# Reordering loads, state updates and the last copies in the SSD layer of a two-layer decoder step

## The reference

```python
def ssd_mixer(h, conv_state, ssm_state, ...):
    proj = h @ w_in                       # z (2048), xbc (3072), dt (32)
    conv = silu(conv_b + sum_k xpad[:, k:k + t] * conv_w[k])
    dt = softplus(dt_raw + dt_bias)
    # per chunk and head: decay from cumsum(dt * a), y = (C B^T * decay) @ (x dt) + C state
    new_state = state * exp(cum[:, -1]) + einsum('bsgrp,bsgn->bgrpn', xdt * to_end, bm)
    y = (y + d_skip * xs) * silu(z)
    y = y * rsqrt(mean(y * y, -1) + 1e-5) * norm_g      # mean over each of 4 groups of 512
    return y @ w_out, new_conv_state, new_state
```

## Time and profile before

| what | value |
|---|---|
| median of 3 runs | 1172.66 us |
| runs | 1162.14 to 1172.76 us |
| the profiled execution | 1171.1 us, span 1169.3 us |
| PE busy | 1051.3 us (90%) |
| DVE / ACT / POOL busy | 469.3 / 297.0 / 133.3 us |
| mean granted TensorE clock | 0.945 |
| SSD stage | 0 to 300 us |
| tail 0, from norm to gated embedding | 300 to about 617 us |

### The profile page before, as it was taken

How to read it: one execution, slowest core, us unless ns; L and a number is a source line. 1 busy time by engine, 2 the same in 40 slices (tenths; PEclk the granted TensorE clock), 3 DMA queues, 4 the chain that set the end, 5 groups by cost and what they waited for, 6 DMA issues and landing times. The chain is left out here.

```text
span 1169.3 us, 14744 instructions
## 1 busy us (share of the span) xinstructions
PE 1051.3 (90%) x5243; PEld 658.4 (56%) x5243; DVE 469.3 (40%) x1383; ACT 297.0 (25%) x765; POOL 133.3 (11%) x121
## 2 busy tenths in 40 slices
PE   7899998698799999899799989779989999989868
PEld 5688775587554444344477875345755344444347
DVE  2769898932331112011355977472161111111132
ACT  2211798700321111111220015362051011101031
POOL 0000013300001000000004724452000000000000
PEclk9899998799988999999999998889988999999989
DMA  8744696675959999999556975949368899999901
GB/s 287 248 163 149 220 278 215 198 281 198 399 225 408 427 429 428 425 427 428 213 216 235 339 262 178 370 136 382 128 265 370 363 427 426 428 428 426 417 4 38
DMA packets 88943, 347.36 MB, mean 297 GB/s; under 512 B 14690, under 2 KB 52578, under 8 KB 72322
## 3 DMA queue, kind: packets, MB, share of 16 engines
q1 hardware_dynamic: 81186, 313.57, 69.3%
q10 hardware_dynamic: 5376, 24.40, 5.3%
q0 software_dynamic: 2304, 8.39, 1.8%
HBM read 331.66 MB, written 23.04 MB: 303 GB/s over the span
## 5 line engine op out<-in xcount | busy, mean ns | idle before, releaser
L1097 PE MATMUL mh<-expert_ring,x_packed 128*64 128x512 f32 x768 | 173.0, 606 | 14.6 <-DMA expert_ring<-in_moe_w_up 12.7
L1349 DVE TENSOR_TENSOR hid<-mh,silu_gate 128x512 f32<-128x512 f32 x16 | 11.1, 692 | 374.8 <-PE mh L1097 325.9
L1097 PEld LDWEIGHTS mh<-expert_ring,x_packed 128*64 128x64 f32 x768 | 58.2, 140 | 126.3 <-issue 124.3
L1119 PE MATMUL mo<-expert_ring,hid_T 128*64 128x512 f32 x384 | 89.1, 618 | 1.4 <-ACT hid_T L1218 1.4
L495 PE MATMUL ss<-xT,expert_ring 128*128 128x264 f32 x384 | 90.0, 395 | 0.0
L1563 PE MATMUL na<-xT,expert_ring 128*128 128x264 f32 (+1 forms) x336 | 78.8, 398 | 6.1 <-DMA expert_ring<-in_nsa_w_in 3.3
L495 PEld LDWEIGHTS ss<-xT,expert_ring 128*128 128x128 f32 x384 | 73.8, 195 | 13.8 <-issue 0.8
L1563 PEld LDWEIGHTS na<-xT,expert_ring 128*128 128x128 f32 (+1 forms) x336 | 64.6, 193 | 20.2 <-DMA expert_ring<-in_nsa_w_in 4.1
L506 PE MATMUL ss<-xT,expert_ring 128*128 128x264 f32 x256 | 64.1, 406 | 6.1 <-ACT z L385 6.1
L1179 PE MATMUL mg<-acc,expert_ring 128*128 128x264 f32 x256 | 61.7, 406 | 7.2 <-ACT acc L883 7.2
L1097 PE MATMUL mh<-expert_ring_more,x_packed 128*64 128x512 f32 x256 | 58.3, 609 | 7.7 <-DMA expert_ring_more<-in_moe_w_up 3.6
(11 more groups left out here) (377 smaller groups left out, 1541.1 us busy)
## 6 DMA issues: line engine op xcount, KB each, us to landing
expert_ring<-in_moe_w_down SPq DMA_DIRECT2D x24, 2048.0 KB, 22.3
expert_ring<-in_moe_w_gate SPq DMA_DIRECT2D x24, 2048.0 KB, 17.2
expert_ring<-in_moe_w_up SPq DMA_DIRECT2D x24, 2048.0 KB, 23.5
expert_ring<-in_ssd_w_in SPq DMA_DIRECT2D x10, 2048.0 KB, 7.9
expert_ring_more<-in_moe_w_gate SPq DMA_DIRECT2D x8, 2048.0 KB, 14.7
expert_ring_more<-in_moe_w_up SPq DMA_DIRECT2D x8, 2048.0 KB, 19.2
expert_ring_more<-in_moe_w_down SPq DMA_DIRECT2D x8, 2048.0 KB, 22.5
expert_ring<-in_cmp_pages SPq DMA_DIRECT2D x40, 256.0 KB, 4.5
```

What stands on the lines that cost most here:

```text
L1097: last = mm(hb[w][s * CAP:(s + 1) * CAP, :], xg[:, k, s * CAP:(s + 1) * CAP], unit(6 * i + 2 * w + s)[:, k * FF:(k + 1) * FF], start=k == ...
L1119: last = mm(ob[2 + a][s * CAP:(s + 1) * CAP, :], ht[:, k, s * CAP:(s + 1) * CAP], unit(6 * i + 4 + s)[:, o:o + 512], start=k == 0, stop=k ...
L1349: V.tensor_tensor(hid[:], hb[1][:], sg[:], ALU.mult).then_inc(hid_ok, 1)
```

## The change

1. `xT` and the first weight chunk are loaded in halves, each half on its own semaphore. PE starts with the first four of the eight products of conv tiles 1 to 3, then waits for the second half of `xT` and for `wdt`, does the `dt` projection, and finishes tiles 1 to 3.
2. ACT and DVE wait for four constants only (`ld_first`) before `dt`; the other eleven are issued behind weight chunk 1 and waited for at `turn_dt` and in DVE behind conv tile 6. Weight chunk 2 goes behind them and ahead of `pos_w`.
3. The `pos_w` softmax leaves the start: DVE's first two instructions go behind conv tile 12, ACT's exponential behind the last `silu`, DVE's last three behind the state updates.
4. State updates 21 to 31 (11 groups, 44 instructions) go behind `normalize(3)`; before, 21 to 26 stood in the last two pairs, 27 ahead of `normalize(0)` and 28 to 31 ahead of `normalize(3)`. The gated decode columns move ahead into the last pair.
5. `load_w(7)` becomes two loads of 0.5 MB into `cbuf` and into the first part of `mm_` (through `w_row`), when the last state is read and when the last pair's product is done. In SP's list they stand ahead of `store_state(5)`.
6. The `win_old` copy leaves ACT's queue and becomes SP's last load issue of the second tail (L == 1), waited for at the very end.

```diff
-            w_at = [ring[:, 1, 0:2048]] + [wk[c][:, h * 2048:(h + 1) * 2048] for c in (1, 2, 0) for h in range(2)] + [ring[:, 1, 2048:CH]]
+            w_at = [ring[:, 1, 0:2048]] + [wk[c][:, h * 2048:(h + 1) * 2048] for c in (1, 2, 0) for h in range(2)]
+            w_row = lambda k: w_at[k // 2][:, (k % 2) * D:(k % 2 + 1) * D] if k < JX - 2 else (cbuf[:].rearrange("p a n -> p (a n)"), work[:, 0:D])[k % 2]
...
-            new_by = [min(2 * i, 16) if i < 9 else 16 + i - 8 if i < 14 else 21 + 3 * (i - 13) for i in range(NPAIR)]
+            new_by = [min(2 * i, 16) if i < 9 else min(16 + i - 8, 21) for i in range(NPAIR)]
...
-                    sp.dma_start(xT[:], I["xT"].rearrange("(k p) t -> p k t", p=P)).then_inc(ld_x, 16)
+                    x_src = I["xT"].rearrange("(k p) t -> p k t", p=P)
+                    sp.dma_start(xT[:, 0:4, :], x_src[:, 0:4, :]).then_inc(ld_x, 16)
+                    sp.dma_start(wk[0][:, 0:2048], I["ssd_w_in"][wk_src[0]][:, 0:2048]).then_inc(ld_half, 16)
+                    sp.dma_start(xT[:, 4:8, :], x_src[:, 4:8, :]).then_inc(ld_x2, 16)
                     sp.dma_start(wdt.rearrange("p k n -> p (k n)"), I["ssd_w_dt"]).then_inc(ld_dt, 16)
-                    load_wk(0)
-                    for dst, name in ((convp, "conv_params"), (taps[:, :, 0:3, :], "conv_state"),
-                                      (ident[:], "ident"), (ones[:], "ones"), (m384[:], "m384"), (lnp[:], "lnp"),
+                    sp.dma_start(wk[0][:, 2048:CH], I["ssd_w_in"][wk_src[0]][:, 2048:CH]).then_inc(ld_wk[0], 16)
+                    for dst, name in ((heads[:], "heads"), (ones[:], "ones"), (convp, "conv_params"), (taps[:, :, 0:3, :], "conv_state")):
+                        sp.dma_start(dst, I[name]).then_inc(ld_first, 16)
+                    load_wk(1)
+                    for dst, name in ((ident[:], "ident"), (m384[:], "m384"), (lnp[:], "lnp"),
...
+                    load_wk(2)
                     sp.dma_start(wb[:], I["pos_w"]).then_inc(ld_pos, 16)
                     sp.dma_start(ptab[:], I["page_table"]).then_inc(ld_pos, 16)
-                    load_wk(1)
-                    load_wk(2)
...
                     load_w(5)
                     load_w(6)
+                    sp.wait_ge(dec_read, JX * DB)
+                    sp.dma_start(w_row(JX - 2), I["ssd_w_out"][7][:, 0:D]).then_inc(ld_w[7], 16)
+                    sp.wait_ge(y_done, NH)
+                    sp.dma_start(w_row(JX - 1), I["ssd_w_out"][7][:, D:2 * D]).then_inc(ld_w[7], 16)
                     store_state(5)
                     load_b(sp, 7)
                     store_state(6)
-                    sp.wait_ge(st_out[2], 32)
-                    load_w(7)
...
-                    act.wait_ge(pos_d, 1)
-                    A(wb[:], wb[:], ACT.Exp).then_inc(pos_a, 1)
-                    act.wait_ge(ld_const, 16 * 15)
+                    act.wait_ge(ld_first, 64)
...
                     silu(JC)
+                    act.wait_ge(pos_d, 1)
+                    A(wb[:], wb[:], ACT.Exp).then_inc(pos_a, 1)
                     take_z(0)
...
-                    act.dma_start(O["win_old"], I["cache_win"][:, 1:, :]).then_inc(win_out, 16)
...
                     pe.wait_ge(ld_x, 16)
+                    pe.wait_ge(ld_half, 16)
+                    for m in range(1, 4):
+                        conv_tile(m, range(4))
+                    pe.wait_ge(ld_x2, 16)
                     pe.wait_ge(ld_dt, 16)
...
-                        conv_tile(m)
+                        conv_tile(m, range(4, KD) if m < 4 else range(KD))
...
+                        if i == NPAIR - 1:
+                            dve.wait_ge(z_silu, 2)
+                            V.tensor_tensor(c3, c3, zs[:, :, SEQ:T], ALU.mult).then_inc(s_gated, 1)
...
                     dve.wait_ge(s_sum, 1)
-                    add_state(27)
                     normalize(0)
                     normalize(1)
                     normalize(2)
-                    for t in range(28, NPC):
+                    normalize(3)
+                    for t in range(21, NPC):
                         add_state(t)
-                    normalize(3)
+                    dve.wait_ge(pos_a, 1)
+                    dve_step(dve, V.tensor_reduce(wst[:], wb[:], AX.X, ALU.add))
+                    dve_step(dve, V.reciprocal(wst[:], wst[:]))
+                    V.tensor_tensor(wb[:], wb[:], wst[:].unsqueeze(2).to_broadcast([P, 4, BLK]), ALU.mult)
...
                             load_unit(sp, L, n, unit(n))
+                        if L == 1:
+                            sp.dma_start(O["win_old"], I["cache_win"][:, 1:, :]).then_inc(win_out, 16)
```

More of the change, by code:

```diff
@@ L140, in trunk @@
         over_sems = [[sem(f"over{L}_{n}") for n in ("ld", "dve", "pe", "act")] for L in range(2)]
+        win_out = sem("win_out")
         ssd_sems = []
@@ L209, in trunk @@
             read_by = [min(NPC, 8 + 3 * (i + 1) // 2 if i < 8 else 20 + 2 * (i - 7)) for i in range(NPAIR)]
[L210 to L212 removed]
+            new_by = [min(2 * i, 16) if i < 9 else min(16 + i - 8, 21) for i in range(NPAIR)]
+            (ld_x, ld_x2, ld_half, ld_first, ld_dt, ld_pos, ld_hsel, pos_d, pos_a, pads, dt_abs, dt_ready, da_ready, conv_done, silu_done, conv_out,
              tr_done, tr_taken, cum_pe, cum_ready, exp_pe, ex_ready, bc_pe, bc_rows_out, yd_ready, cb_done, cb_ready, bc_done, seg_done, exp_done, w_done,
              y_done, y_taken, xe_ready, st_done, st_taken, dec_read, new_state, sd_scaled, z_done, z_taken, z_silu, y_gated, sq_done, s_sq,
[L215 removed]
+             sq_sum, s_sum, s_gated, ms_done, sqrt_done, y_ready, w_read) = (
                 stage_sem("s_" + n) for n in (
[L217 removed]
+                    "ld_x", "ld_x2", "ld_half", "ld_first", "ld_dt", "ld_pos", "ld_hsel", "pos_d", "pos_a", "pads", "dt_abs", "dt_ready", "da_ready", "conv_done", "silu_done", "conv_out",
                     "tr_done", "tr_taken", "cum_pe", "cum_ready", "exp_pe", "ex_ready", "bc_pe", "bc_rows_out", "yd_ready", "cb_done", "cb_ready", "bc_done", "seg_done", "exp_done", "w_done",
                     "y_done", "y_taken", "xe_ready", "st_done", "st_taken", "dec_read", "new_state", "sd_scaled", "z_done", "z_taken", "z_silu", "y_gated", "sq_done", "sample_sq",
[L220 removed]
+                    "sq_sum", "sample_sum", "sample_gated", "ms_done", "sqrt_done", "y_ready", "w_read"))
             ld_wk = [stage_sem(f"s_ld_wk{c}") for c in range(3)]
@@ L331, in _ @@
                     sp.wait_ge(conv_out, 32)
-                    sp.wait_ge(win_out, 16)
                 @block.gpsimd
@@ L485, in _, with conv_tile @@
                     tri = m384[:, 0:P]
-                    def conv_tile(m):
+                    def conv_tile(m, ks=range(KD)):
                         c, s = (m - 1) // 4, ((m - 1) // 4) % 3
-                        if m % 4 == 1:
+                        if m % 4 == 1 and ks[-1] == KD - 1:
                             pe.wait_ge(ld_wk[s], 16 * (c // 3 + 1))
@@ L493, in conv_tile @@
                         wc = wk[s].rearrange("p (k n) -> p k n", k=KD)
-                        for k in range(KD):
+                        for k in ks:
                             last = mm(pt[m % 4][:, 0:T], wc[:, k, ((m - 1) % 4) * P:((m - 1) % 4 + 1) * P], xT[:, k, :], start=k == 0, stop=k == KD - 1)
-                        last.then_inc(tile_done, 1)
+                        if ks[-1] == KD - 1:
+                            last.then_inc(tile_done, 1)
                     def z_tile(j):
@@ L510, in turn_dt @@
                         pe.wait_ge(dt_ready, 1)
+                        pe.wait_ge(ld_const, 16 * 11)
                         for q in range(QT):
@@ L607, in out_part @@
                             if m == 0 and k % 2 == 0:
-                                pe.wait_ge(ld_w[k // 2], 16)
-                            last = mm(o_bank[m][:, 0:T], w_at[k // 2][:, (k % 2) * D + m * P:(k % 2) * D + (m + 1) * P], cv[:, k, :],
+                                pe.wait_ge(ld_w[k // 2], 16 if k < JX - 2 else 32)
+                            last = mm(o_bank[m][:, 0:T], w_row(k)[:, m * P:(m + 1) * P], cv[:, k, :],
                                       start=k == 0, stop=k == JX - 1)
@@ L773, in _ @@
                             V.tensor_copy(dtat[:], aux[:, 2 * NH:4 * NH].rearrange("p (q h) -> p q h", q=QT).unsqueeze(2).to_broadcast([P, QT, 2, NH])).then_inc(tr_taken, 1)
+                            dve.wait_ge(ld_const, 16 * 11)
                         elif m == 8:
@@ L784, in _ @@
                             V.tensor_tensor(bcp[:], cv[:, JX:JX + NG, SEQ:T], cv[:, JX + NG:JC, SEQ:T], ALU.mult).then_inc(bc_pe, 1)
+                        elif m == 12:
+                            dve.wait_ge(ld_pos, 32)
+                            dve_step(dve, V.tensor_reduce(wst[:], wb[:], AX.X, ALU.max))
+                            V.tensor_tensor(wb[:], wb[:], wst[:].unsqueeze(2).to_broadcast([P, 4, BLK]), ALU.subtract).then_inc(pos_d, 1)
```

(1 more changed line is left out.)

17 lines of the change are left out of this document (2 added, 15 removed).

## The result

The changed kernel takes 1182.01 us (median; 1176.94 to 1197.26), the kernel before 1168.08 us on the same chip: ratio 1.0117, 95% interval 1.0094 to 1.0140; the ratio leaves out one execution of the 20, 1197.26 us, as one in a slower state. It is slower by 1.2%, 13.9 us. The forecast was 1175.0 us and 1161 to 1181; the time lies 1 us above its range. The likeliest of its cases, a change of less than 1%, is missed by 2 us, with an interval that still reaches down to 0.94%. The profiled execution after is 1184.8 us (span 1183.0, mean granted clock 0.935) against 1171.1, so the two profiles differ by 13.7 us and may be read against each other.

What follows compares the result with a forecast made beforehand. The prediction took PE, busy 90% of the span, and expert loads at full DMA rate as bounds; the change shifts when PE reaches the experts. 1171.1 us plus 3.5 gave 1174.6, predicted as 1175, range 1161 to 1181.

Steps and rivals of the forecast that it cites:

- The sum: At the experts: +2.8 us from late wple, -0.8 of the ranks' wait, +1.5 for low clock, together +3.5 us.
- The start: Start of the SSD stage: earlier dt and a possible clock gain bring 4.3 us (2 to 5.2) at the sums.
- The chain behind it is unchanged: ACT, DVE and six convolutions after dt stay as before, so PE's wait at the sums shrinks to about 0.7 us.
- The clock, two chances in three: Behind the wait at the cumulative sums: full clock would gain 2.6 us, at two chances in three 1.8 us.
- The norm: Without the updates ahead of the gated columns, mean squares and output product start 2.1 us sooner.
- The DMA line: From store_state(5) at 269.4 us: 20.0 us of transfers plus 2.3 for its ends, unit 5 issued at 291.7.
- the side sum: DVE's own path (store, B row, four groups of updates) would let state 7 be issued at 282.4 us.
- The stage's end: At PE the SSD stage ends 6.4 us sooner, at 293.2 us instead of 299.6.
- What a wait costs beyond itself: After PE's 9 us wait at project(0): 8 records at 1.2 GHz cost 1.5 us, ranks' own wait saves 0.8.
- The copy: win_old behind the last gate units ends at 1147 to 1156 us, covered by the last output store at 1167.2.
- (a): Rival: the DMA line is shorter, PE passes project(0) with half or all the stage's gain; 1164 to 1171; chance 0.32.
- (b): Rival: start waits as before plus 0.9, or sums keep the clock low; 2 us less gained, 1177; within forecast's 0.55.

Runs made afterwards that it cites:

- the run with the copy alone: The kernel before with part 6 alone (win_old copied on SP's queue behind the second tail's last units): 1167.51 us, ratio 0.9993.
- the run with the updates alone: The kernel before with parts 4 and 5 alone (late updates, earlier gated columns, last weight piece in halves): 1180.31 us, ratio 1.0122.
- the last run: The changed kernel with updates 21 to 31 ahead of normalize(3), table load ahead of ACT's wait, project(0) and project(1) behind ranks and first slot product: 1171.09 us, ratio 1.0010.

## Why the prediction was wrong, by its own steps

The mechanism of the loss was the one forecast: stores late, unit 5 late, `wple` late, PE waits for it, more lost than gained. What failed are sizes: above all the price of the wait (+0.7 us taken, +5.2 measured), then the gain of the start (4.3 us taken, 1.8 at the sums, because of a table load behind a wait), then the length of the DMA line (22.3 us taken, 24.2 measured). The sum stood at +3.5 us at the experts and came out at +13.1 (the second pair).

**The start: 4.3 us taken, 1.8 measured at the sums, 0.4 at 134 us and 1.9 at the last pair.** PE's start (7.2, measured 7.14) and `dt` done (18.1, measured 17.8) were right, the second with some luck: with the same first instructions it was done at 17.7 to 19.6 us in nine profiles. "The chain behind it is unchanged" was not: I moved the softmax away from ACT's start "with a table load that is only moved" and did not ask which instruction then becomes the first with a table to load, behind which wait. The wait at the sums is 2.28 instead of 0.7 us; 1.28 of that is the load, as the run with the load ahead of the wait shows, and at 134 us it had cost some 3 us (133.80 and 130.81 above). The clock, two chances in three, did not come: 0.59 and 0.55 in the windows at 40 and 44 us, 0.58 and 0.56 before. With a wait of 1 us half of the gain came in one run (0.58, then 0.99) and all of it in another. That 1.9 us stood at the last pair (217.68 against 219.59) is not the work of the start: 1.5 of it came at 181 us, where the 16 records behind a wait of 3.9 us took 5.36 us after and 6.81 before, and the run with the copy alone, whose start is the old one, has 5.21 there. The price of the load stands in the Trainium skill as well ("ScalarE: Activation LUTs", section "What ACT_TABLE_LOAD costs": some 1283 ns, and a drain of 1380 ns with it). The trace agrees on the first, 1.28 us; of a drain it shows nothing, as `dt` starts 1.30 us after the load began.

**The norm: 2.1 us, right** (the wait ahead of the mean squares 3.31 and 1.06 us, a gain of 2.2; group 3's chain 4.15 as before). The products of `state` behind it were 0.4 us slower. Together with the start the output product came 3.8 us earlier, not 6.4, so `store_state(5)` was issued at 272.04, not 269.4: **2.6 us**.

**The DMA line: 22.3 us taken, 24.2 measured, 1.9 more**; and from unit 5 to `wple` 32.7 and 33.2, 0.5 more. These three give 5.0 us, and `project(0)` came at 329.45 where the sum had 324.4. The line was made of transfers that fill the engines without a gap, 20.0 us of them, and 2.3 for its two ends. That picture holds in the trace: they are full from 273 to 294 us, 1 to 1.5 us longer than taken, and the ends make up the rest. State 7's issue was paced by DVE and its B row, at 284.07 where the side sum had 282.4, but the engines had work meanwhile. What the line is worth shows where unit 4 and the prompt store were taken out of it: unit 5 went out 7.9 us sooner, and about half of the loss was gone.

**The stage's end: PE was put at 293.2; it was SP that came last.** The sum took PE's products as the pace. It ends when all engines are through, and SP's list was part of the late line: PE was done at 295.8, the norm began at 299.14. It should have cost nothing by itself, since `wple` was late anyway (this is argued, no run shows it), but a reader of the profile should have PE's 7.44 us of wait and 3.35 of block end together: 10.8 us of PE without work, 9 forecast.

**What a wait costs beyond itself: +0.7 taken (1.5 for the clock less 0.8 of another wait), +5.2 measured.** From `project(0)` to the first expert 19.4 us instead of 17.1 (2.3), to the down product 2.3 more (the light block 8.89 in place of 6.55 us before), to the second pair 0.6. I had priced the low clock for the 8 records right behind the wait (1.94 for them) and for nothing that came later. This 4.5 us and the 5.0 above are the whole difference of the sum, 13.1 less 3.5, within 0.1. It is the largest term that was mis-sized, but how much of it the wait caused is open. The 1.94 us came again in the run with the updates alone (3.89 us behind a wait of 9.74). The later loss did not: from `project(0)` to the second pair that run takes 53.7 us, 2.8 more than before, and after takes 56.1. The light block takes 7.21 us there, 6.55 before, and 8.26 in the last run, which had no wait for `wple` at all:

```profile
363.41 7.21 PE L1060 MATMUL mo<-token_and_gates,slot_onehot 128*128 128x17 f32 x42
...
347.21 8.26 PE L1072 MATMUL mo<-token_and_gates,slot_onehot 128*128 128x17 f32 x42
```

After, the windows from 350 to 362 us are at 1.00, so the engine had been back at full clock for 12 us before this block fell to 0.50.

**The copy: right.** Its traffic falls off at about 1162 us, 1147 to 1156 forecast, with the whole tail 13.7 us late, and that is some 18 us ahead of the issue of the last output store, 11 forecast; its cost is below what can be measured. The prediction weighed a rule of the Trainium skill ("DMA: Bandwidth & Descriptors", section "Why a DMA increments its semaphore by 16 and not by 1"), by which a DMA of outer size 8 is spread over 8 engines. The trace agrees: a share of 0.51 at 222 GB/s in the windows at 1155 us. The first output store took 5.8 us to landing beside it, 2.1 before; whether it stood behind the copy in a queue or only shared the engines with it is not shown.

**Rivals and range.** (a), a shorter line, was given 0.32; the trace has a longer one, and no kernel with all eleven groups late escaped the wait. (b), little gained from the start, ended nearest to the measured time (1177), and half of its cause was the right one: the low clock at the sums stayed. The range ended at these cases, 1181. For what follows 9 us of wait it allowed nothing above the 1.5 us taken, though rows of before had slow light work in the same stretch: 0.34 us for a record of the projections against 0.24 in a warm tile.

## What to carry to other kernels

Ask of each update moved off an engine's path which queue waits for its result, and walk that queue to the next thing that the slow engine needs. A late store is free only until the point at which the buffers behind it come free: here unit 5 issued at 279 us cost nothing that could be measured, at 288 0.5% and at 296 1.2%. When an instruction leaves an engine's start, look which one becomes first and whether it carries a table load behind a wait. And give a long wait on TensorE a price beyond its length: behind 7.4 and 9.7 us of wait the next 8 records took 1.9 us more. Behind 2.0 us they took 1.3 more and behind 2.8 us 0.1 more, so no fixed sum can be carried over, and what comes later than those records is not shown to be its doing.

## What the runs showed that I had not expected

- The first 24 records of the start took 6.96, 7.00, 7.00, 7.46, 8.13, 8.14, 8.27, 8.51 and 8.64 us in nine runs with the same first instructions. They are slow at first and then quick, and how long the slow part lasts differs between executions; the windows from 7 to 17 us, read in three of these profiles (7.00, 8.64 and 6.96 us), give a granted clock of 1.00 throughout, so the cause is open. It moved the sums from 40.4 to 42.3 us in kernels whose start is the same. Before, the wait for constants hid it: 42.2 to 42.3 us in three profiles. The changed start lets it through.
- The same 24 records of the projections take 5.61 us in three profiles, 7.2 to 7.4 in three and 8.1 to 8.4 in four, the before and the after among the last: the clock there is worth up to 3 us, with no difference in the code.
- The NSA stage, the same code in all, is 219.1 to 227.8 us long from run to run (222.6 before). Gains of 3 to 7 us at the first expert disappear in that; what it hangs on was not tried.
- An issue on SP can take long by itself: 4.26 us for unit 4 and 6.00 us for state 7 behind other stores, in place of 0.4. In the run with unit 4 first, where fewer bytes stood ahead, the stores were issued in 0.4 us each. What holds the issue is not shown.
